# Fewer and larger visits of attention's own products between the weight units of a hybrid decoder layer

## What is computed

```
h  = rms_norm(x)
qkv, gates = split(h @ w_in)                      # 2048 -> 3608 + 3 * 2048
y_a = sliding-window attention (8 heads of 64, sinks, ALiBi)
y_b = stick-breaking attention (4 heads of 128, strictly causal)
y_c = native sparse attention (8 heads of 64): compressed + selected + window branches
merged = sum over a, b, c of sigmoid(g_i) * (y_i @ w_branch_i)
x  = x + merged @ w_out
h  = rms_norm(x);  x = x + (silu(h @ w_gate) * (h @ w_up)) @ w_down
out = rms_norm(x)
```

## Time and profile before

| | |
|---|---|
| median of 3 runs | 1362.46 us (1362.15 to 1363.37) |
| the profiled execution's own time | 1363.83 us |
| its span, first to last instruction | 1362.1 us |
| TensorE matmul busy | 1350.7 us (99%) |
| TensorE weight loads busy | 1315.9 us (97%) |
| VectorE busy | 950.6 us (70%) |
| ScalarE busy | 712.1 us (52%) |
| mean granted TensorE clock | 0.999 of full |
| mean memory rate | 190 GB/s |

### The profile page before, as it was taken

The page is one execution under the profiler, slowest core; times in us unless marked ns, Lnnn a source line. Parts: engine busy times, 40 slices in busy tenths (PEclk is TensorE's granted clock), DMA queues, the critical chain, the costliest instruction groups (busy, mean ns, idle before and its releaser), DMA issues.

```text
span 1362.1 us, 26444 instructions
## 1 busy us (share of the span) xinstructions
PE 1350.7 (99%) x11247; PEld 1315.9 (97%) x11247; DVE 950.6 (70%) x1241; ACT 712.1 (52%) x927; POOL 44.8 (3%) x70
## 2 busy tenths in 40 slices
PE   8999999999999999999999999999999999999997
PEld 7888999999999999999999999999999999999997
DVE  6554456667654756767899899985546899988554
ACT  6333356656545664455655655544344555555444
POOL 3000010000000110000000000000000000000111
PEclk9999999999999999999999999999999999999999
DMA  7776555544565667555566666656556666666653
GB/s 244 248 229 223 181 170 156 155 140 141 156 188 167 194 204 225 182 187 171 185 194 197 220 195 190 198 197 208 199 189 189 196 214 191 194 192 230 211 194 124
DMA packets 135264, 261.08 MB, mean 192 GB/s; under 512 B 8448, under 2 KB 25408, under 8 KB 134768
## 3 DMA queue, kind: packets, MB, share of 16 engines
q1 hardware_dynamic: 132912, 251.13, 57.8%
q0 software_dynamic: 1792, 7.57, 1.6%
q10 hardware_dynamic: 448, 0.76, 0.2%
HBM read 257.33 MB, written 2.10 MB: 190 GB/s over the span
## 4 chain that ended last, share of the span: by engine, by line
PE 98%; DMA 1%; DVE 0%; ACT 0%; issue 0%; ACTq 0%; DVEq 0%
PE bank L649 26%; PE bank L651 25%; PE bank L650 25%; PE bank L888 5%; PE bank L891 5%; PE bank L890 5%; PE bank L637 3%; PE bank L787 1%; PE bank L698 1%; DMA raw_ring<-in_w_in 0%; DMA sigmoid_gates<-in_norm_mix 0%; PE bank L747 0%; PE bank L1011 0%; PE bank L699 0%; PE bank L835 0%; PE bank L813 0%
## 5 line engine op out<-in xcount | busy, mean ns | idle before, releaser
L1327 DVE TENSOR_TENSOR weight_lo_ring<-raw_ring,weight_hi_ring 128x1024 fp32r<-128x1024 f32 (+2 forms) x479 | 582.3, 1221 | 317.9 <-ACT weight_hi_ring L1071 260.4
L1071 ACT ACTIVATE weight_hi_ring<-raw_ring 128x1024 fp32r<-128x1024 f32 (+2 forms) x431 | 450.6, 1050 | 459.3 <-PE bank L651 299.5
L649 PE MATMUL bank<-weight_hi_ring,hT_hi 128*128 128x256 f32 (+2 forms) x1276 | 380.9, 298 | 0.0
L651 PE MATMUL bank<-weight_hi_ring,hT_lo 128*128 128x256 f32 (+2 forms) x1276 | 375.5, 294 | 0.0
L650 PE MATMUL bank<-weight_lo_ring,hT_hi 128*128 128x256 f32 (+2 forms) x1276 | 375.5, 294 | 0.0
L649 PEld LDWEIGHTS bank<-weight_hi_ring,hT_hi 128*128 128x128 f32 x1276 | 239.8, 188 | 10.0 <-issue 3.4
L650 PEld LDWEIGHTS bank<-weight_lo_ring,hT_hi 128*128 128x128 f32 x1276 | 239.9, 188 | 6.1
L651 PEld LDWEIGHTS bank<-weight_hi_ring,hT_lo 128*128 128x128 f32 x1276 | 239.6, 188 | 6.3
L649 PE MATMUL bank<-weight_hi_ring,h2T_hi 128*128 128x256 f32 x704 | 195.5, 278 | 0.0
L650 PE MATMUL bank<-weight_lo_ring,h2T_hi 128*128 128x256 f32 x704 | 194.6, 276 | 0.0
L651 PE MATMUL bank<-weight_hi_ring,h2T_lo 128*128 128x256 f32 x704 | 194.6, 276 | 0.0
(11 more groups left out here) (253 smaller groups left out, 1933.5 us busy)
## 6 DMA issues: line engine op xcount, KB each, us to landing
raw_ring<-in_w_in SPq DMA_DIRECT2D x96, 512.0 KB, 3.5
raw_ring<-in_w_gate SPq DMA_DIRECT2D x88, 512.0 KB, 4.3
raw_ring<-in_w_up SPq DMA_DIRECT2D x88, 512.0 KB, 4.2
raw_ring<-in_w_down SPq DMA_DIRECT2D x88, 512.0 KB, 4.0
raw_ring<-in_w_in SPq DMA_DIRECT2D x55, 480.0 KB, 4.2
raw_ring<-in_w_out SPq DMA_DIRECT2D x32, 512.0 KB, 4.0
raw_ring<-in_w_br_c SPq DMA_DIRECT2D x16, 256.0 KB, 3.8
raw_ring<-in_w_br_a SPq DMA_DIRECT2D x16, 256.0 KB, 6.5
```

The lines of the kernel that those rows point to most:

```text
L649: pe.matmul(dst, x_hi, w_hi, start=opening, stop=False, skip_group_check=True)
L651: m = pe.matmul(dst, x_lo, w_hi, start=False, stop=last and k == UK - 1, skip_group_check=True)
L1071: act.activation(whi[:, s, :, 0:width(u)], raw[:, s, :, 0:width(u)], ACT.Copy)\
L1327: dve.tensor_tensor(lo, w, hi.bitcast(F32), ALU.subtract).then_inc(lo_ready, 1)
```

## The change

It moves the visits' contents between slots and gives the values another place. It does not alter what is computed, nor the weight units.

- The values' result goes to the free columns 384 to 511 of the score banks, first token tile to bank 4, second to bank 5. For that `values` makes three matmuls of 128 columns for each head where it made one of 256 and one of 128. VectorE reads the result in two halves of 128 columns where it read one of 256.
- Transposes of probabilities move from 5 to 6 slots after their scores, values from 6 to 9, so both fall into slots that have scores. In a slot TensorE now does values, preparation, scores, transposes, stick.
- `PREP` slots are paired: 1, 3, 5, 35, 60 and 63 do two each, 36 one; the compression starts at slots 3 and 5.
- The stick heads' steps are 0, 6 and 12 slots from their start, in place of 0, 5 and 9.
- `merge_T_at` puts two column blocks of `merged` into one slot (118 and 122), in banks 4 to 7.
- Waits follow: values wait for the scores of all earlier slots and for the preparations of all earlier slots (both use banks 4 and 5), and for the reading of the values before; transposes no longer wait for `values_read`, except after the compressed step.

```diff
-MLP_AT = [4, 6]
+MLP_AT = [3, 5]
-PROBS_T_AT = {soft_slot(i) + 5: i for i in range(N_SOFT)}
-VALUES_AT = {soft_slot(i) + 6: i for i in range(N_SOFT)}
+PROBS_T_AT = {soft_slot(i) + 6: i for i in range(N_SOFT)}
+VALUES_AT = {soft_slot(i) + 9: i for i in range(N_SOFT)}
-PREP = [(0, "c", KCMP, 0), (1, "c", VCMP, 1), (2, "q", QC, 0), (3, "q", QC, 1), (4, "k", KSEL, 0), (5, "k", KWIN, 1),
+PREP = [(1, "c", KCMP, 0), (1, "c", VCMP, 1), (3, "q", QC, 0), (3, "q", QC, 1), (5, "k", KSEL, 0), (5, "k", KWIN, 1),
-    for _s in (0, 5, 9):
+    for _s in (0, 6, 12):
-    return BRANCH_END[2 * NC_D + m] + LAG
+    return BRANCH_END[2 * NC_D + (m | 1)] + LAG
...
             def values(i, h, v):
 
-                dst = bank[7][HD * h:HD * (h + 1), :]
-                pe.matmul(dst[:, S:2 * S], v[0], pT[:, i % 2, h, 0:S], start=True, stop=False)
-                return pe.matmul(dst[:, S + P:2 * S], v[1], pT[:, i % 2, h, S:3 * P], start=False, stop=True)
+                first, second = (bank[4 + t][HD * h:HD * (h + 1), 3 * P:4 * P] for t in range(TT))
+                pe.matmul(first, v[0], pT[:, i % 2, h, 0:P], start=True, stop=True)
+                pe.matmul(second, v[0], pT[:, i % 2, h, P:S], start=True, stop=False)
+                return pe.matmul(second, v[1], pT[:, i % 2, h, S:3 * P], start=False, stop=True)
...
+                if k in VALUES_AT:
+                    i = VALUES_AT[k]
+                    kind, pr = soft(i)
+                    pe.wait_ge(probsT, i + 1)
+                    if i >= 1:
+                        pe.wait_ge(values_read, i)
+                    pe.wait_ge(scores_sb, SOFT_BY[k])
+                    pe.wait_ge(prep_done, PREP_BY[k])
...
-                        pe.wait_ge(values_read, i)
+                        pe.wait_ge(probsT, i)
+                    if i == CMP + 1:
+                        pe.wait_ge(values_read, i)
...
-                            if n >= UPC + 2:
-                                pe.wait_ge(t_lo, n - 1)
+                            if m >= 2:
+                                pe.wait_ge(t_lo, n - 3)
+                            elif m == 1:
+                                pe.wait_ge(values_read, N_SOFT + SB_HEADS)
```

More of the change, by code:

```diff
@@ L166 @@
 SOFT_AT = {soft_slot(i): i for i in range(N_SOFT)}
-PROBS_T_AT = {soft_slot(i) + 5: i for i in range(N_SOFT)}
-VALUES_AT = {soft_slot(i) + 6: i for i in range(N_SOFT)}
-PREP = [(0, "c", KCMP, 0), (1, "c", VCMP, 1), (2, "q", QC, 0), (3, "q", QC, 1), (4, "k", KSEL, 0), (5, "k", KWIN, 1),
-        (34, "q", QA, 0), (35, "q", QA, 1), (36, "k", KA, 0),
-        (50, "sq", QB, 0), (51, "sq", QB, 1), (52, "sk", KB, 0), (53, "sk", KB, 1)]
-PREP_AT = {p[0]: n for n, p in enumerate(PREP)}
+PROBS_T_AT = {soft_slot(i) + 6: i for i in range(N_SOFT)}
+VALUES_AT = {soft_slot(i) + 9: i for i in range(N_SOFT)}
+SOFT_BY = {k: sum(soft_slot(i) < k for i in range(N_SOFT)) for k in VALUES_AT}
+PREP = [(1, "c", KCMP, 0), (1, "c", VCMP, 1), (3, "q", QC, 0), (3, "q", QC, 1), (5, "k", KSEL, 0), (5, "k", KWIN, 1),
+        (35, "q", QA, 0), (35, "q", QA, 1), (36, "k", KA, 0),
+        (60, "sq", QB, 0), (60, "sq", QB, 1), (63, "sk", KB, 0), (63, "sk", KB, 1)]
+PREP_AT = {k: [n for n, p in enumerate(PREP) if p[0] == k] for k in {p[0] for p in PREP}}
+PREP_BY = {k: sum(p[0] < k for p in PREP) for k in VALUES_AT}
 NSA_GATES_SLOT = 3
@@ L695, in values @@
             def values(i, h, v):
-                dst = bank[7][HD * h:HD * (h + 1), :]
-                pe.matmul(dst[:, S:2 * S], v[0], pT[:, i % 2, h, 0:S], start=True, stop=False)
-                return pe.matmul(dst[:, S + P:2 * S], v[1], pT[:, i % 2, h, S:3 * P], start=False, stop=True)
+                first, second = (bank[4 + t][HD * h:HD * (h + 1), 3 * P:4 * P] for t in range(TT))
+                pe.matmul(first, v[0], pT[:, i % 2, h, 0:P], start=True, stop=True)
+                pe.matmul(second, v[0], pT[:, i % 2, h, P:S], start=True, stop=False)
+                return pe.matmul(second, v[1], pT[:, i % 2, h, S:3 * P], start=False, stop=True)
             def mixer_step(k):
-                if k in PREP_AT:
-                    p = PREP_AT[k]
+                if k in VALUES_AT:
[6 more added lines that the diff above has]
+                    pe.wait_ge(prep_done, PREP_BY[k])
+                    if kind == "cmp":
+                        for pr in range(PAIRS):
+                            m = pe.matmul(bank[7 - pr // 2][:, (pr % 2) * S:(pr % 2 + 1) * S],
+                                          vz[:, 2 * pr:2 * pr + 2, :].rearrange("p h d -> p (h d)"),
+                                          pT[:, i % 2, 0, 0:S], start=True, stop=True)
+                    else:
+                        for h in range(2):
+                            c = {"sel": VSEL, "win": VWIN, "swa": VA}[kind] + HD * h
+                            m = values(i, h, [proj[:, t, c:c + HD] for t in range(TT)])
+                    m.then_inc(values_full, 1)
+                for p in PREP_AT.get(k, []):
                     _, what, col, b = PREP[p]
@@ L806, in mixer_step @@
                     m.then_inc(probsT_full, 1)
[L807 to L816, removed]
-                        for h in range(2):
-                            c = {"sel": VSEL, "win": VWIN, "swa": VA}[kind] + HD * h
-                            m = values(i, h, [proj[:, t, c:c + HD] for t in range(TT)])
-                    m.then_inc(values_full, 1)
                 for h, s in STICK.get(k, []):
@@ L1631, in read_values @@
                 dve.wait_ge(values_full, i + 1)
-                src = bank[7][:, S:2 * S]
-                if kind == "sel":
-                    last = dve.tensor_copy(yacc[:, pr, :], src)
-                elif kind == "win":
-                    last = dve.tensor_tensor(yacc[:, pr, :], src, yacc[:, pr, :], ALU.add)
-                elif kind == "swa":
-                    last = split_y(1, pr, src)
+                if kind != "cmp":
+                    for t in range(TT):
+                        src, tokens = bank[4 + t][:, 3 * P:4 * P], slice(t * P, (t + 1) * P)
+                        if kind == "sel":
+                            last = dve.tensor_copy(yacc[:, pr, tokens], src)
+                        elif kind == "win":
+                            last = dve.tensor_tensor(yacc[:, pr, tokens], src, yacc[:, pr, tokens], ALU.add)
+                        else:
+                            last = split_y(1, pr, src, tokens)
                 else:
@@ L1648, in mixer_step @@
                     return
-                if k in PREP_AT:
-                    prepare(PREP_AT[k])
+                for p in PREP_AT.get(k, []):
+                    prepare(p)
                 if k == 1:
```

26 lines of the change are left out of this document (14 added, 12 removed).

## The result

| | before | changed |
|---|---|---|
| median | 1362.41 us (1362.15 to 1364.51, 10 runs) | 1365.74 us (1365.19 to 1367.51, 10 runs) |
| ratio | | 1.0022, 95% interval 1.0014 to 1.003 |
| profiled execution's span | 1362.1 us | 1363.8 us |
| visits between slots 0 and 122 | 56 | 32 |
| their prices, summed | 60.10 us | 61.61 us |

A forecast was written before the change was run, and what follows sets the result against it. TensorE's own stream was taken to bound the kernel. The terms -0.67 - 0.69 + 0.21 = -1.15 us, against the median of 1362.46 us, gave 1361.3 us, with a range of 1359.6 to 1364.0.

The forecast's parts named there:

- unit 82: Weight unit whose low part might come late for TensorE, margin 0.2 us, cost at most 0.3 us; rival's chance 0.1.
- units 108 to 111: Branch-weight units that the later reload of x might delay, cost at most 0.5 us; rival's chance 0.1.
- (1): Pairing of tokens: two visits become one behind unit 1, the wait for VectorE falls away; -0.67 us.
- (2): Fewer visits in the weight stream: 23 others vanish, each saving a cheap crossing of 0.03 us; -0.69 us.
- (3): Scores and values share a visit in seven slots, eight before: +0.21 us; new order taken as the old one's.
- (4): Values steps: three matmuls for two in each head, twelve steps; taken as 0, bounds 0 and 1.8 us.
- The first rival: Values steps: the two heads no longer overlap; +2.6 us, net 1364.0, or 1369 in strict order; chance 0.12.
- milder case: Values steps: head 1 starts two records late, 0.22 us x 12 = +2.6 us, giving 1364.0 us.
- (5): VectorE reads values in halves, ScalarE and VectorE steps move to other slots, new waits of TensorE; cost 0.
- rows of two for L700: Values' rows in the profile: twice two records instead of one row of four if the heads don't overlap.
- 2.8: Visit of values, scores and transposes, forecast at 2.55 us: over 2.8 or under 2.3 us the prediction is wrong.
- theory E: Expectation for a follow-up run: a visit's end decides the weight stream's cadence behind it; stage some 410.0 us.

The follow-up runs named there:

- c_prep2: The kernel before with only preparations, compression and merged blocks grouped, softmax, values and stick heads as before; 1364.88 us, ratio 1.0011.
- a_inter: The changed kernel with the values' six matmuls taken in turn from the two heads; 1367.49 us, ratio 1.0027.
- c_tfirst: a_inter with the transposes ahead of values and scores in each slot; 1363.57 us, ratio 0.9999.
- b_three: The kernel before with values in three matmuls of 128 columns for each head, head by head, in bank 7; 1366.98 us, ratio 1.0024.
- b_three_inter: b_three with the values' matmuls taken in turn from the two heads; 1366.32 us, ratio 1.0025.
- d_last: b_three_inter with only the last step's values as in the kernel before, two matmuls for each head; 1363.65 us, ratio 1.0001.
- c_rep: a_inter with the last of the six transposes of probabilities done twice in each of twelve steps; 1366.51 us, ratio 1.0022.
- d_one: a_inter with only the last step's values head by head; 1364.06 us, ratio 1.0006.
- d_mix: c_tfirst with slot 15's transposes behind the scores again and the youngest stick head first in slots with several; 1362.63 us, ratio 0.9992.

## Why the prediction was wrong

Point by point:

- **What bounds the kernel:** right. TensorE's stream sets the end, and no wait of it appeared, not at unit 82 nor at units 108 to 111.
- **(1) Pairing of tokens, -0.67 us:** right; measured 2.05 to 1.30, -0.75 us, alone (c_prep2) and in the changed kernel.
- **(2) 0.03 us for each other visit that vanishes:** right; 0.04 measured in c_prep2. Transposes behind values and scores do a little better: with the values in turn (a_inter) that visit cost 2.49 us against 1.89 + 0.69 apart, 0.09 less; ahead of them it is 2.54, 0.04 less.
- **(3) Values ahead of scores:** right. 2.54 us for six transposes, values and scores in c_tfirst is 0.66 + 1.88, so the new order shares a crossing as the old one did.
- Without term (4) the prices come to 58.47 - 60.10 = -1.63 us (a_inter), where the forecast had -1.15.
- **(4) Values in three matmuls for two, taken as 0 with bounds of 0 to 1.8 us:** this is the step that failed. It measured 61.61 - 58.47 = 3.14 us in the changed kernel and 63.21 - 60.10 = 3.11 us by itself (b_three), 0.26 us for each of twelve steps. I priced a matmul's length and asked whether a small one streams as well as a large one. It does: the same three matmuls in turn cost nothing (60.22 against 60.10, b_three_inter). What changed was how many records stand between the first matmuls of the two column halves. Both bounds were worked out from lengths, so the true value lay outside them.
- **The first rival had the mechanism,** with the decisive point named, at a chance of 0.12 and +2.6 us. The argument against it, that a depth of four costs nothing now, was no argument, since the change made it six. Its milder case is what came: head 1 starts two records late, when three of head 0's six are left. Only the size was off, 0.27 us for these two records and not 0.22. Of the signs named beforehand, the rows of two for L700 came, while the visit's 2.75 us stayed just under the 2.8 that was to mark a failure. The 0.27 us give 1361.3 + 3.2 = 1364.5 us, already over the range.
- **(5) Waits, VectorE, ScalarE: 0.** Right.
- **The cadence was in no term.** The forecast counted the stream between visits at one pitch, 0.1135 us. It has two, and the changed order puts 312 more matmuls of the stage on the slower one: 1.39 us. 1364.5 less the 0.5 us by which the other prices did better than forecast, plus 1.4, is 1365.4 us; measured 1365.7.

The range itself has a slip: its lower end of 1359.8 was put down as 1359.6, which changes nothing here.

That the prices add up, and that a single late half and the cadence are the whole loss of the stage, is shown by the table and by b_three, b_three_inter and d_last. What decides which cadence a visit leaves behind is open. It is the same in two executions of one program; it does not hang on what the visit ends with alone (c_tfirst, against theory E); a change of 0.1 us in a visit alters it there and at visits long after (c_rep, d_one). The stretch before a visit has a part: in a_inter the five like visits of slots 18 to 30 leave slow, fast, slow, fast, slow, each the other cadence than the one that it was entered with. That fits a phase of some nanoseconds between two parts of TensorE at the restart, which no row shows, so it stays argued. Nor is it settled why the 229 matmuls from 682 us on are slow in most profiles and fast in those of the changed kernel, a_inter, d_last and d_mix; the executions without a profile can't be asked, and so the 1.0 us there is left out of the sum against the medians.

## What to carry to other kernels

Where two tiles of the array are meant to work side by side, write their matmuls in turn; splitting each tile's work into more matmuls, tile by tile, can put the second tile out of reach at no change in columns. Price a split by order, not by length. And in a stream that TensorE bounds, sum the visits and the pitch of the stream apart: a reordering that saves a microsecond of visits can lose two in the pitch, and only a measured version tells.

## What the runs showed of the hardware

- TensorE starts a matmul of the free column half ahead of waiting ones of the other half, when at most three records of those (or one whole matmul) are still to start. With the six head by head, head 1 starts at 375.64 us, ahead of head 0's L702 at 375.86. The Trainium skill (TensorE: Matmul & The Clock Gate, The mechanism) states that matmuls start strictly in program order; the rows disagree, and by that rule the kernels with values in turn and head by head would have cost alike.
- The stream of 128x256 matmuls with a weight load each has two stable pitches at full clock, 0.1133 and 0.1178 us, 4% apart. In the stage either holds from one visit to the next, for 520 steps in a row in b_three_inter and d_last, whatever the other engines do meanwhile; behind it one change comes without a visit, at 682 us in the kernel before, where the products of the weight sums end. In both, the weight load's record starts right behind the start of a matmul and lasts 0.19 us, so what is longer in the slow one shows in no record. Weight loads of the changed kernel, slow and then fast:

```profile
347.49 0.19 PEld L652 LDWEIGHTS bank<-weight_lo_ring,yT_hi 128*128 128x128 f32 x1
347.61 0.19 PEld L653 LDWEIGHTS bank<-weight_hi_ring,yT_lo 128*128 128x128 f32 x1
347.73 0.19 PEld L651 LDWEIGHTS bank<-weight_hi_ring,yT_hi 128*128 128x128 f32 x1
...
239.48 0.19 PEld L651 LDWEIGHTS bank<-weight_hi_ring,hT_hi 128*128 128x128 f32 x1
239.60 0.19 PEld L652 LDWEIGHTS bank<-weight_lo_ring,hT_hi 128*128 128x128 f32 x1
239.71 0.19 PEld L653 LDWEIGHTS bank<-weight_hi_ring,hT_lo 128*128 128x128 f32 x1
```
